# Layer 1's output projection: half of its inputs by seven products of block pairs for eight

## The chip, the cores and the metric

One core of one Trainium2 chip runs the whole kernel. The metric is the device time of one execution in microseconds. The engines are PE (TensorE, matmuls), PEld (its weight loads), DVE (VectorE), ACT (ScalarE), POOL (GpSimd) and SP (SyncE, which here only issues DMAs).

## What is computed

Two layers on x (1024 positions by 1024 channels), then a final RMSNorm. The change lies in layer 1, the pooling mixer, and there in its last product:

```python
def odd_mixer(h, w_in, w_grp, b_grp, scale, w_out):
    proj = h @ w_in                      # 1024 -> 2 * 2048
    v, g = jnp.split(proj, 2, axis=-1)
...
    mixed = jnp.einsum('bsgc,gcd->bsgd', pooled - vg, w_grp).reshape(bsz, s, POOL_WIDTH) + b_grp
    y = mixed * scale * jax.nn.silu(g)
    return y @ w_out                     # (1024 x 2048) @ (2048 x 1024)
...
        x = x + gate[:, None, :] * y
    return rmsnorm(x, final_g)
```

y has four groups of four blocks of 128 channels. Below, block k of y is y[:, 128 k : 128 (k + 1)], held with its channels on the 128 partitions.

## The kernel before, in words

**Precision.** Every large product of float32 operands is made of three matmuls in float32r: each operand is split into an upper part (ACT, a copy that rounds, `..._hi`) and a lower part (DVE, operand less upper part, `..._lo`), and hi·hi, hi·lo and lo·hi are summed in PSUM (`products`, L2190 to L2195). "A matmul" below is one of the three, 128x128 by 128x512.

**Seven products.** Most of the input projections are already made by pairs of column blocks with a scheme of seven products for eight (`pair`, `product`): the 1024 inputs are halved into even and odd 128-blocks (4 of each, KP = 4), the 1024 positions into two halves. The moving side X, in SBUF for the whole layer, holds four blocks of h and three sums T1, T2, T3 (T4 takes B12's place later), each hi and lo. The stationary side of a pair comes from two loaded blocks of weights (`R1`, `R2`): POOL makes four sums (`sums_of_weights`), ACT and DVE split them (`prep(q, idx)`, in slots of a ring w_hi/w_lo of six 512-wide places). A product is 4 x 3 = 12 matmuls. Product 4 of a pair runs after product 1 of the next (`last_of`). ACT and DVE add up the products from PSUM (`take_1`, `add_11` and so on).

**Layer 1's output projection.** The 16 blocks of y are written to DRAM (`spill_y`) as the four groups are finished, in the order 0, 3, 2, 1. Then come two passes, A over the row blocks b = 0 to 3 and B over b = 4 to 7. A pass has 16 steps, one for each block k of y: SP loads 128 rows of w_out into the ring `raw` (`ring_load`, four places) and half of block k of y (`y_load`), ACT and DVE split both (`step_splits`), and PE runs 4 row blocks x 2 halves of the columns x 3 matmuls = 24 matmuls, y stationary, the weights moving. All eight PSUM banks gather a pass. The last two steps of pass A (three of pass B) are run row block by row block, so that the banks fill one after the other. `residual(1, b)` (DVE) multiplies a row block by the gate and adds it to x, four operations of 512 columns for a row block; `squares`, `inverse` and `row_out` make the final norm; `store` writes the rows.

**What sets the order.** All engines run instruction lists written out by hand, with semaphores. Every engine takes its list in order, so that what waits holds back all behind it. A split may be made when its ring place is free: the place of step n's weights is that of step n - 3 (`E_LAST`, `w_used`), and y's upper part has three places (YS). PE counts `o_step` at the last row block of a step. In pass A of before DVE's list at the turn to pass B reads:

```python
                        if layer == 1 and p == "B":
                            if at == 1:
                                residual(1, 0)
                                residual(1, 1)
                                residual(1, 2)
                            if at == 2:
                                residual(1, 3)
                        step_splits(y_step)
```

Of the kernel before, what the change touches and what calls it, by code (L numbers as in the profile page):

```python
# [10 lines left out]
P = 128  # L11
# [8 lines left out]
GB = 4  # L20
# [20 lines left out]
for _name, _n in ROWS_A + ROWS_B:  # L41
# [14 lines left out]
PAIRS += [(name, n) for n in range(GROUPS) for name in ("V01", "G01", "V23", "G23") if n or name[1] == "2"]  # L56
Q = {pair: q for q, pair in enumerate(PAIRS)}

# [6 lines left out]
        if PAIRS[q] != ("C", HEADS - 1) and not (PAIRS[q][0] == "V01")}  # L65
TIME_ORDER = [k + half * KB for k in range(KB) for half in range(2)]
GROUP_ORDER = [GB * g + m for g in GORDER for m in range(GB)]
# [3 lines left out]
           1: {b: (2 * (b % 4), 2 * (b % 4) + 1) for b in range(SB)}}  # L71
# [39 lines left out]
def build(nc, x, c, norm_g, mod_w, mod_b, hy_w_in, hy_conv_w, hy_conv_b, lru_w_a, lru_b_a, lru_w_x, lru_b_x,  # L111
# [41 lines left out]
    def last_steps(layer, p):  # L153


        blocks, steps = BLOCKS[layer, p], list(range(2 * KB - LAST[layer, p], 2 * KB))
# [30 lines left out]
    for q in range(3 * (HEADS - 1)):  # L187
        add_pair(q)
    STEPS = [(layer, p, k) for layer, p in BLOCKS
             for k in ((TIME_ORDER if layer == 0 else GROUP_ORDER) if p == "A" else range(2 * KB))]  # L190
    mods1 = [("m1", chunk, kk) for kk in range(KB) for chunk in range(2)]
    for layer in range(2):
        if layer == 1:
# [38 lines left out]
    with ExitStack() as ctx:  # L232
# [67 lines left out]

        def flat(ap):
# [55 lines left out]
        def piece(at, width, dt=F32):  # L357
            if dt is F32R:
# [124 lines left out]
        half_done = sem("half_done")  # L483

# [53 lines left out]
        def dst_free(q, which):  # L538
# [28 lines left out]
        def _(sp):  # L567
# [25 lines left out]
            def ring_load(unit):  # L593
# [9 lines left out]
                if kind in ("R1", "R2"):  # L603
                    name, n = PAIRS[unit[1]]
                    which = "R1 R2".split().index(kind)
                    if name in PAIR_L0:
# [44 lines left out]
            def y_load(step):  # L651
# [3 lines left out]
                if Y[step] >= YR:  # L655
                    sp.wait_ge(ylo_done, Y[step] - YR + 1)
                if p == "A":
# [1920 lines left out]
```

## Time and profile before

| | us |
|---|---|
| median of 3 runs | 1303.23 |
| lowest and highest run | 1301.58, 1304.64 |
| the profiled execution, its own time | 1303.3 |
| its span in the trace | 1301.5 |
| PE busy | 1278.2 (98%) |
| DVE, ACT, POOL busy | 938.1, 629.3, 273.0 |

The span begins with the first instruction and ends with the last store; the execution's own time is 1.8 us more. In the page PE's busy time counts a matmul of 512 columns as 0.39 us, though the next one starts 0.227 us after it: they overlap, so the pace is read from starts and not from durations. A row of a timeline gives the start, the duration, the engine, the line, and in brackets how long the engine was idle before it and what ended that.

### The profile page before, as it was taken

How to read it: one execution, taken by the hardware profiler on the slowest of the kernel's cores; microseconds unless marked ns; L12 is line 12 of the kernel's file. 1: busy time of each engine (PE TensorE's matmuls, PEld its weight loads, DVE VectorE, ACT ScalarE, POOL GpSimd, SP SyncE). 2: the span in 40 equal slices, each digit the busy share in tenths (PEclk: the TensorE clock that was granted, in tenths of full speed). 3: DMA queues.
4: the chain of work that ended last, by engine and by line, in shares of the span. 5: the costliest groups of instructions: out<-in, count | busy, mean ns of one | idle time of the engine just before them, and what ended most of it. 6: DMA issues, size and time to landing. Idle time of an engine off the chain costs nothing.

```text
span 1301.5 us, 15429 instructions
## 1 busy us (share of the span) xinstructions
PE 1278.2 (98%) x5687; PEld 1055.3 (81%) x5687; DVE 938.1 (72%) x1119; ACT 629.3 (48%) x888; POOL 273.0 (21%) x158
## 2 busy tenths in 40 slices
PE   6999999999999999999999999999999999999997
PEld 5877888888888888888888888888888888888886
DVE  6889987878878887778477698758758656434636
ACT  7466656464646464545567574144144143222522
POOL 0033443443524332000000023133133131000000
PEclk8999999999999999999999999999999999999999
DMA  9712233323232341698748202321321321874441
GB/s 290 218 49 69 89 110 97 104 67 113 69 114 73 110 134 45 223 380 269 268 165 267 81 18 79 101 79 34 112 82 34 112 81 39 309 243 145 177 155 65
DMA packets 145618, 171.51 MB, mean 132 GB/s; under 512 B 6598, under 2 KB 117382, under 8 KB 145544
## 3 DMA queue, kind: packets, MB, share of 16 engines
q1 hardware_dynamic: 145544, 170.53, 40.6%
q8 instruction: 46, 0.75, 0.2%
q14 instruction: 28, 0.23, 0.1%
HBM read 145.33 MB, written 25.17 MB: 131 GB/s over the span
## 4 chain that ended last, share of the span: by engine, by line
PE 88%; DVE 7%; SPq 2%; issue 1%; ACT 1%; DMA 0%; DVEq 0%; ACTq 0%
PE psum L2193 29%; PE psum L2195 29%; PE psum L2194 29%; SPq L587 1%; DVE whole_x L1863 1%; DVE w_lo L1410 1%; DVE X L1500 1%; PE psum L2328 1%; DMA late<-in_mod_w 0%; SPq L576 0%; ACT w_hi L879 0%; DVE bufs L1645 0%; DVE w_lo L1432 0%; DVE late L1493 0%; PE psum L2334 0%
## 5 line engine op out<-in xcount | busy, mean ns | idle before, releaser
L2193 PE MATMUL psum<-X,w_hi 128*128 128x512 f32 x1140 | 446.3, 391 | 2.6 <-DVE X L1544 2.2
L2194 PE MATMUL psum<-X,w_hi 128*128 128x512 f32 x1140 | 444.4, 390 | 0.0
L2195 PE MATMUL psum<-X,w_lo 128*128 128x512 f32 x1140 | 444.3, 390 | 0.0
L2193 PEld LDWEIGHTS psum<-X,w_hi 128*128 128x128 f32 x1140 | 214.5, 188 | 49.4 <-DVE X L1544 2.8
L2195 PEld LDWEIGHTS psum<-X,w_lo 128*128 128x128 f32 x1140 | 214.4, 188 | 44.9
L2194 PEld LDWEIGHTS psum<-X,w_hi 128*128 128x128 f32 x1140 | 214.5, 188 | 44.3 <-issue 0.2
L1410 DVE TENSOR_TENSOR w_lo<-raw,w_hi 128x1024 fp32r<-128x1024 f32 x98 | 120.5, 1231 | 156.4 <-ACT w_hi L879 156.0
L879 ACT ACTIVATE w_hi<-raw 128x1024 fp32r<-128x1024 f32 x98 | 103.6, 1057 | 201.6 <-PE psum L2195 159.9
L901 ACT ACTIVATE w_hi<-ssum 128x512 fp32r<-128x512 f32 x140 | 87.1, 626 | 120.3 <-PE psum L2195 91.1
L1432 DVE TENSOR_TENSOR w_lo<-ssum,w_hi 128x512 fp32r<-128x512 f32 x140 | 119.9, 863 | 22.1 <-ACT w_hi L901 21.4
L840 POOL TENSOR_TENSOR ssum<-raw 128x512 f32<-128x512 f32 x35 | 62.6, 1790 | 287.5 <-DMA raw<-in_pool_w_in 253.7
L848 POOL TENSOR_TENSOR ssum<-ssum,raw 128x512 f32<-128x512 f32 x35 | 55.8, 1595 | 309.4 <-DVE w_lo L1432 309.4
L2193 PE MATMUL psum<-w_hi,X 128*128 128x512 f32 x256 | 99.7, 389 | 0.3 <-DVE whole_x L1867 0.3
L2195 PE MATMUL psum<-w_hi,X 128*128 128x512 f32 x256 | 99.6, 389 | 0.0
L2194 PE MATMUL psum<-w_lo,X 128*128 128x512 f32 x256 | 99.6, 389 | 0.0
L851 POOL TENSOR_TENSOR ssum<-raw 128x512 f32<-128x512 f32 x35 | 78.5, 2244 | 78.7 <-DVE w_lo L1432 78.7
L845 POOL TENSOR_TENSOR ssum<-ssum,raw 128x512 f32<-128x512 f32 x35 | 62.1, 1774 | 47.1 <-DVE w_lo L1432 45.1
L1424 DVE TENSOR_TENSOR w_lo<-raw,w_hi 128x1024 fp32r<-128x1024 f32 x35 | 42.7, 1220 | 24.7 <-ACT w_hi L890 24.5
L2193 PEld LDWEIGHTS psum<-w_hi,X 128*128 128x128 f32 x256 | 48.0, 188 | 10.7 <-DVE whole_x L1867 0.7
L2195 PEld LDWEIGHTS psum<-w_hi,X 128*128 128x128 f32 x256 | 48.0, 188 | 10.0
L2194 PEld LDWEIGHTS psum<-w_lo,X 128*128 128x128 f32 x256 | 48.0, 188 | 9.9
L2193 PE MATMUL psum<-d_hi,w_hi 128*128 128x512 f32 x128 | 49.9, 390 | 0.3 <-DVE w_lo L1410 0.3
(244 smaller groups left out, 1955.0 us busy)
## 6 DMA issues: line engine op xcount, KB each, us to landing
raw<-in_hy_w_in SPq DMA_DIRECT2D x48, 512.0 KB, 5.2
raw<-in_hy_w_out SPq DMA_DIRECT2D x48, 512.0 KB, 4.9
raw<-in_pool_w_in SPq DMA_DIRECT2D x32, 512.0 KB, 5.1
raw<-in_pool_w_out SPq DMA_DIRECT2D x32, 512.0 KB, 4.1
aux<-in_mod_w SPq DMA_DIRECT2D x16, 512.0 KB, 4.0
y_dram<-bufs SPq DMA_DIRECT2D x16, 512.0 KB, 2.6
raw<-in_mod_w SPq DMA_DIRECT2D x16, 512.0 KB, 5.9
y_dram<-gb_ SPq DMA_DIRECT2D x16, 512.0 KB, 3.3
```

The lines of the kernel that those rows point to most:

```text
L840: nc.gpsimd.tensor_tensor(even, a21, a22, ALU.add).then_inc(s_ready, 1)
L845: nc.gpsimd.tensor_tensor(odd, even, a11, ALU.add).then_inc(s_ready, 1)
L848: nc.gpsimd.tensor_tensor(even, odd, a12, ALU.add).then_inc(s_ready, 1)
L851: nc.gpsimd.tensor_tensor(odd, a21, a11, ALU.add).then_inc(s_ready, 1)
L879: nc.scalar.activation(flat(w_hi[:, es:es + 2, :]), raw[:, at, :], ACT.Copy).then_inc(hi_done, 1)
L901: nc.scalar.activation(w_hi[:, es, :], ssum[:, op % 2, :], ACT.Copy).then_inc(hi_done, 1)
L1410: nc.vector.tensor_tensor(flat(w_lo[:, es:es + 2, :]), raw[:, at, :], flat(w_hi[:, es:es + 2, :]).bitcast(F32), ALU.subtract).then_inc(lo_ ...
L1424: ins = nc.vector.tensor_tensor(w_lo[:, es:es + 2, :].rearrange("p two (k n) -> p two k n", k=KP), raw_blocks(q, 0), w_hi[:, es:es + 2, :] ...
L1432: ins = nc.vector.tensor_tensor(w_lo[:, es, :], ssum[:, op % 2, :], w_hi[:, es, :].bitcast(F32), ALU.subtract)
L2193: nc.tensor.matmul(out_, whi, xhi, start=first, stop=False, skip_group_check=check)
L2194: nc.tensor.matmul(out_, whi, xlo, start=False, stop=False, skip_group_check=check)
L2195: return nc.tensor.matmul(out_, wlo, xhi, start=False, stop=last, skip_group_check=check)
```

## The change

Layer 1's output projection is split by inputs. Blocks k = 0 to 3 and 12 to 15 of y (the two groups that are finished first) go on as steps, so that each pass has 8 steps. Blocks 4 to 11 go by four pairs of row blocks (`("O", j)`, j = 0 to 3, rows 256 j to 256 j + 255) with the scheme of seven products. The stationary side is now y (R1 and R2 are two row blocks of the eight y blocks, read back from DRAM), and the moving side are 1024 rows of w_out, loaded into X's place when h is no longer needed, with the same seven blocks. The pairs run between pass A and pass B. Pair j yields rows 2j and 2j + 1 complete over these inputs; `add_rows` multiplies them by the gate and adds them to x's rows. What the two passes yield is added by `residual` as before.

With it goes: POOL makes T1 and T3 of the resident weights and DVE T2 and T4 (8 operations each, 512 wide); ACT and DVE split them in eight operations each, 2048 and 1536 wide (`upper_out`, `low_out`), put between the splits of pass A's steps; y's halves get places of their own (`y_raw1`, `y_hi1`, and `y_lo1` in y_raw1's place), so `y_load` waits for PE to have used a place (`o_step`) and no longer for DVE; SP loads the eight blocks of w_out (512 KB each) after the weights of the steps 1 and 2; the spills of the last group, the gate's row and x's rows move.

```diff
-GROUP_ORDER = [GB * g + m for g in GORDER for m in range(GB)]
+GROUP_ORDER = [GB * g + m for g in GORDER[:2] for m in range(GB)]
+PAIRED = range(GB, GB + KB)
+N_STEPS = (2 * KB, KB)
...
@@ SP
+            def out_weights(kp):
+                sp.wait_ge(full_of["4"], OUT)
+                for n in range(2):
+                    k = PAIRED[2 * kp + n]
+                    sp.dma_start(whole_x[kp][:, 2 * n:2 * n + 2, 1, :],
+                                 w_out[1][k * P:(k + 1) * P, :].rearrange("p (two n) -> p two n", two=2))\
+                      .then_inc(out_in[kp], 16)
+            for n, step in enumerate(s for s in STEPS if s[0] == 1 and s[1] == "A"):
                 ring_load(("W",) + step)
                 y_load(step)
+                if n in (1, 2):
+                    for kp in (2 * n - 2, 2 * n - 1):
+                        out_weights(kp)
...
@@ ACT
+            for n, step in enumerate(s for s in STEPS if s[0] == 1 and s[1] == "A"):
+                if n < 2:
+                    continue
+                step_splits(step)
+                if n in (2, 3, 4, 5):
+                    upper_out(n - 2)
+            load_root()
+            first_operands(OUT)
...
@@ DVE
+            for n, step in enumerate(s for s in STEPS if s[0] == 1 and s[1] == "A"):
+                if n < 2:
+                    continue
+                step_splits(step)
+                if n in (2, 3, 4, 5):
+                    t2_and_t4_out(n - 2)
+                    if n > 2:
+                        low_out(n - 3)
+            low_out(KP - 1)
+            first_operands(OUT)
+            residual(1, 0)
+            residual(1, 1)
+            prep(OUT, 0)
+            residual(1, 2)
...
@@ PE
                 if q >= 2:
                     pe.wait_ge(neg21, q - 1)
+                if q == OUT:
+                    pe.wait_ge(out_lo, 2 * KP)
+                    pe.wait_ge(o_evac, o_count(1, 1, 1))
                 product(q, "1")
...
+                if q == OUT:
+                    pe.wait_ge(o_evac, o_count(1, 2, 1))
...
+                if (layer, p) == (1, "B"):
+                    for q in range(OUT, len(PAIRS)):
+                        pair(q, after_1=(lambda: last_of(q - 1)) if q > OUT else None)
```

ACT's list in pass A, before. L879 is the upper split of a step's weights, L946 that of y; o_step is PE's count of finished steps.

```order
L879 ACTIVATE w_hi<-raw 128x1024 [waits psum_full,raw_in2]
L946 ACTIVATE X<-whole_x 128x512 [waits o_step,y_in2]
L879 ACTIVATE w_hi<-raw 128x1024 [waits o_step,raw_in3]
L946 ACTIVATE X<-whole_x 128x512 [waits o_step,y_in3]
L879 ACTIVATE w_hi<-raw 128x1024 [waits o_step,raw_in0]
```

The same place now. L961 and L1030 are the same two splits, L1469 the splits of the resident weights (`upper_out`), which wait for the sums of POOL (t13_added) and DVE (t24_added).

```order
L961 ACTIVATE w_hi<-raw 128x1024 [waits psum_full,raw_in2]
L1030 ACTIVATE y_hi<-y_raw 128x512 [waits gate_done,o_step,y_in2]
L1469 ACTIVATE X<-whole_x 128x4x512 [waits t13_added,t24_added]
L1469 ACTIVATE X<-whole_x 128x3x512
L961 ACTIVATE w_hi<-raw 128x1024 [waits o_step,raw_in3]
L1030 ACTIVATE y_hi<-y_raw 128x512 [waits o_step,y_in3]
L1469 ACTIVATE X<-whole_x 128x4x512 [waits t13_added,t24_added]
```

Two wide operations that wait for DVE now stand between the splits of two steps. On DVE each step's splits are followed by T2 and T4 (L2296, L2300), for which ACT's next wide operations wait, and then by the two wide lower splits of the group before (L2308).

DVE's list at the end of pass A, before (L1863 and L1867 are `residual`, L1410 and L1477 the splits of pass B's steps 0 and 1):

```order
L1410 TENSOR_TENSOR w_lo<-raw,w_hi 128x1024 [waits hi_done]
L1477 TENSOR_TENSOR X<-whole_x,X 128x512 [waits yhi_done]
L1863 TENSOR_TENSOR whole_x<-psum,whole_x 128x512 [waits psum_full,gate_in]
L1867 TENSOR_TENSOR whole_x<-whole_x 128x512 [waits xr_in0,part_made]
L1863 TENSOR_TENSOR whole_x<-psum,whole_x 128x512 [waits psum_full]
L1867 TENSOR_TENSOR whole_x<-whole_x 128x512 [waits xr_in0,part_made]
```

And now (L1546 and L1554 are the lower splits of operands 0 and 2 of the first pair, L1985 and L1989 `residual`):

```order
L1546 TENSOR_TENSOR w_lo<-raw,w_hi 128x1024 [waits hi_done]
L1554 TENSOR_TENSOR w_lo<-ssum,w_hi 128x512 [waits hi_done]
L1985 TENSOR_TENSOR d_sums<-psum,d_sums 128x512 [waits psum_full,gate_in]
L1989 TENSOR_TENSOR gb_<-gb_,d_sums 128x512 [waits xr_in0,part_made]
L1985 TENSOR_TENSOR d_sums<-psum,d_sums 128x512 [waits psum_full]
L1989 TENSOR_TENSOR gb_<-gb_,d_sums 128x512 [waits xr_in0,part_made]
```

The split of operand 2 now stands ahead of the first `residual`. By the ring (`E_LAST`) operand 2 takes the place of the weights of step 6, the last but one of pass A, so that its upper part waits for PE's count of that step.

## Rows read from the trace of the kernel before

**Rows 1.** The page, parts 1 and 4: busy time, and the chain by engine
```profile
PE 1278.2 (98%) x5687; PEld 1055.3 (81%) x5687; DVE 938.1 (72%) x1119; ACT 629.3 (48%) x888; POOL 273.0 (21%) x158
...
PE 88%; DVE 7%; SPq 2%; issue 1%; ACT 1%; DMA 0%; DVEq 0%; ACTq 0%
```

**Rows 2.** Windows: us of each engine (instructions), clock, DMA share, GB/s
```profile
1110.00:1197.00 87.00, 87.00 (x385) 72.07 (x384) 32.69 (x36) 26.49 (x34) 0.00 (x0) 1.00 0.68 242
1295.00:1302.00 7.00, 0.00 (x0) 0.00 (x0) 3.53 (x6) 1.44 (x6) 0.00 (x0) 0.63 0.41 160
```

**Rows 3.** PE timeline, last group's mix and product 4: start us, us, what
```profile
1099.80 0.39 PE L2193 MATMUL psum<-X,w_hi 128*128 128x512 f32 x1
...
1102.52 0.39 PE L2193 MATMUL psum<-d_hi,w_hi 128*128 128x512 f32 x1
```

**Rows 4.** ACT timeline, pass A, with idle before and its releaser
```profile
1119.10 1.06 ACT L879 ACTIVATE w_hi<-raw 128x1024 fp32r<-128x1024 f32 x1 [7.81 <-PE psum L2195]
1120.06 0.61 ACT L946 ACTIVATE X<-whole_x 128x512 fp32r<-128x512 f32 x1
1124.54 1.06 ACT L879 ACTIVATE w_hi<-raw 128x1024 fp32r<-128x1024 f32 x1 [3.86 <-PE psum L2195]
```

**Rows 5.** DVE timeline, start of pass A
```profile
1119.04 1.28 DVE L2045 SCALAR_TENSOR_TENSOR gb_<-psum,vec,gb_ 128x1024 f32<-128x1024 f32 x1 [3.76 <-PE psum L2195]
1120.24 1.22 DVE L1410 TENSOR_TENSOR w_lo<-raw,w_hi 128x1024 fp32r<-128x1024 f32 x1
1121.37 0.68 DVE L1477 TENSOR_TENSOR X<-whole_x,X 128x512 fp32r<-128x512 f32 x1
```

**Rows 6.** Line 1493, T2 sums of layer 1: ns min/median/max, first and last start
```profile
L1493 DVE SCALAR_TENSOR_TENSOR d_sums<-d_sums,whole_x x4: 691/691/693, 743.4 to 756.5; 128x512 f32<-128x512 f32 x4
```

**Rows 7.** ACT, DVE and PE timelines, end of pass A and start of pass B
```profile
1205.46 1.06 ACT L879 ACTIVATE w_hi<-raw 128x1024 fp32r<-128x1024 f32 x1 [8.62 <-PE psum L2195]
...
1198.09 0.68 DVE L1863 TENSOR_TENSOR whole_x<-psum,whole_x 128x512 f32<-128x512 f32 x1
...
1203.40 0.68 DVE L1863 TENSOR_TENSOR whole_x<-psum,whole_x 128x512 f32<-128x512 f32 x1
...
1210.42 0.40 PE L2195 MATMUL psum<-w_hi,X 128*128 128x512 f32 x1
1211.08 0.50 PE L2193 MATMUL psum<-w_hi,X 128*128 128x512 f32 x1 [0.27 <-DVE whole_x L1867]
```

**Rows 8.** POOL and DVE timelines, one stretch in which both are busy
```profile
1013.05 1.29 POOL L840 TENSOR_TENSOR ssum<-raw 128x512 f32<-128x512 f32 x1 [10.49 <-DMA raw<-in_pool_w_in]
...
1013.50 1.92 DVE L1410 TENSOR_TENSOR w_lo<-raw,w_hi 128x1024 fp32r<-128x1024 f32 x1 [0.49 <-ACT w_hi L879]
1015.35 0.67 DVE L1461 TENSOR_TENSOR vp<-vp,psum 128x512 f32<-128x512 f32 x1
```

**Rows 9.** Windows (columns as in rows 2) and PE timeline: the clock falls and rises
```profile
22.00:24.00 2.00, 0.72 (x5) 0.72 (x6) 1.41 (x4) 0.00 (x0) 0.00 (x0) 0.92 1.10 312
32.00:34.00 2.00, 2.00 (x6) 1.52 (x6) 1.23 (x6) 1.53 (x2) 0.00 (x0) 0.52 1.18 292
1296.00:1297.00 1.00, 0.00 (x0) 0.00 (x0) 1.00 (x1) 0.81 (x3) 0.00 (x0) 0.92 0.00 0
...
23.28 0.69 PE L2390 MATMUL psum<-ones,macc 128*128 128x1 f32 x4 [2.52 <-DVE macc L1525]
...
29.92 0.79 PE L2193 MATMUL psum<-X,w_hi 128*128 128x512 f32 x1 [0.83 <-DVE X L1544]
...
33.92 0.39 PE L2193 MATMUL psum<-X,w_hi 128*128 128x512 f32 x1
```

**Rows 10.** DMA issues of the page and SP timeline: loads for layer 1's projection
```profile
raw<-in_pool_w_out SPq DMA_DIRECT2D x32, 512.0 KB, 4.1
...
1102.77 0.34 SPq L664 DMA_DIRECT2D whole_x<-y_dram  x1
```

More of the change, by code:

```diff
@@ L153, in last_steps @@
     def last_steps(layer, p):
-        blocks, steps = BLOCKS[layer, p], list(range(2 * KB - LAST[layer, p], 2 * KB))
+        blocks, steps = BLOCKS[layer, p], list(range(N_STEPS[layer] - LAST[layer, p], N_STEPS[layer]))
         order = [(n, b, half) for b in blocks for half in range(2) for n in steps]
@@ L483, in build @@
         half_done = sem("half_done")
+        out_in = [sem(f"out_in{kp}") for kp in range(KP)]
+        out_hi = sem("out_hi")
+        out_lo = sem("out_lo")
+        pair_part = sem("pair_part")
+        pair_added = sem("pair_added")
         def v(name, n=0, count=1):
@@ L654, in y_load @@
                 at = Y[step] % YR
[L655 removed]
+                if Y[step] >= YR and layer == 0:
                     sp.wait_ge(ylo_done, Y[step] - YR + 1)
+                elif layer and Y[step] - YR >= Y[1, "A", GROUP_ORDER[0]]:
+                    sp.wait_ge(o_step, Y[step] - YR + 1)
                 if p == "A":
@@ L945, in split_y @@
                 width = slice(0, cols.stop - cols.start)
-                nc.scalar.activation(Y_HI[layer][n % YS][:, width], Y_RAW[layer][n % YR][:, width], ACT.Copy)\
-                  .then_inc(yhi_done, 1)
+                if (n - Y[1, "A", GROUP_ORDER[0]]) in range(YS):
+                    act.wait_ge(gate_done, GB * GROUPS)
+                nc.scalar.activation(y_hi(step)[:, width], y_raw(step)[:, width], ACT.Copy).then_inc(yhi_done, 1)
             def step_splits(step):
@@ new lines, in low_out, with add_rows @@
+            def low_out(kp):
+                for n, blocks in enumerate((slice(0, 4), slice(4, 7))):
+                    dve.wait_ge(out_hi, 2 * kp + n + 1)
+                    nc.vector.tensor_tensor(X[:, kp, blocks, 1, :], whole_x[kp][:, blocks, 1, :],
+                                            X[:, kp, blocks, 0, :].bitcast(F32), ALU.subtract).then_inc(out_lo, 1)
+            def add_rows(q, which):
+                b = 2 * (q - OUT) + which
+                part = dst(q)[which]
+                if which:
+                    second_complete(q)
+                else:
+                    first_complete(q)
+                nc.vector.tensor_tensor(part, part, gate1, ALU.mult).then_inc(pair_part, 1)
+                dve.wait_ge(pair_part, b + 1)
+                dve.wait_ge(xr_in[b % 4], 16 * (2 + b // 4 + 1))
+                nc.vector.tensor_tensor(XR[1][b], XR[1][b], part, ALU.add).then_inc(pair_added, 1)
@@ new lines, in _ @@
+            last = [s for s in STEPS if s[0] == 1 and s[1] == "B"]
+            for q in range(OUT, len(PAIRS)):
+                if q > OUT:
+                    take_22(q - 1)
+                    prep(q, 0)
+                prep(q, 1)
+                if q == OUT:
+                    residual(1, 3)
+                else:
+                    add_rows(q - 1, 0)
+                prep(q, 2)
+                prep(q, 3)
+                add_11(q)
+                if q > OUT:
+                    add_rows(q - 1, 1)
+                prep(q, 4)
+                prep(q, 5)
+                if q == len(PAIRS) - 1:
+                    step_splits(last[0])
+                add_12(q)
+                prep(q, 6)
@@ L2180, in _ @@
+            take_22(len(PAIRS) - 1)
+            step_splits(last[1])
+            for n, step in enumerate(last):
+                if n < 2:
+                    add_rows(len(PAIRS) - 1, n)
+                else:
+                    step_splits(step)
+                if n in (3, 4, 5, 6):
+                    row_out(n - 3)
             residual(1, 4)
@@ L2551, in _ @@
                     part_of(y_steps[n], b, half)
-                for n in range(ends, 2 * KB):
+                for n in range(ends, N_STEPS[layer]):
                     behind(layer, p, n)
```

198 lines of the change are left out of this document (142 added, 56 removed).

## The prediction

> **What bounds the kernel now.** I read the busy times and the chain first: PE is busy for 98% of the span and makes 88% of the chain that ends last [rows 1]. So a matmul taken away is worth its pace, and anything that makes PE wait costs its full length. The pace comes from the starts: product 4, 12 matmuls, begins at 1099.80 and the next mix at 1102.52 [rows 3], which is 2.72 us, or 0.227 us for a matmul. A step of a pass (24 matmuls) is then 5.44 us, and ACT's first split of a step comes exactly so often, at 1119.10 and 1124.54 [rows 4]. The windows show that in pass A PE runs without a gap (87.00 of 87 us) at full granted clock, with DVE busy for 32.7 us, ACT for 26.5 us and POOL for nothing [rows 2]: there is room beside PE. The one gap near the change is at the first step of pass B: PE starts at 1211.08 where it would have started at 1210.42 + 0.23 [rows 7], so 0.43 us are lost to `residual(1, 3)`.
>
> **What goes.** Half the inputs cost 2 passes x 8 steps x 24 = 384 matmuls; four pairs of 84 make 336. The 48 fewer are worth 48 x 0.227 = 10.9 us. The gap of 0.43 us goes too, since row block 3 is then evacuated long before pass B. Gain: 11.3 us. The tail after the last matmul, in which PE has no work [rows 2], keeps its instructions.
>
> **What comes, first place: pass A.** It starts at 1102.52 + 72 x 0.227 = 1118.84 (three mixes after rows 3) and has 8 steps. Between the splits of two steps ACT now has two wide copies that wait for DVE's T4, DVE's T2 and T4 come behind the step's lower splits, and these wait for ACT. That is a ring of waits, and I add it up:
> - ACT's copies take 0.61 us for 512 and 1.06 us for 1024 columns [rows 4], so 0.45 us for 512 more: 1.96 us for 2048 and 1.51 for 1536. Consecutive ones overlap by 0.1 us (1119.10 + 1.06 against 1120.06). The two wide ones hold ACT for 3.27 us, then the step's weights take 1.06.
> - DVE's splits take 1.73 us from start to the next start (1.13 between rows 5's last two starts, then some 0.6), and T2 and T4, each waiting for the one before, 2 x 0.69 [rows 6] and 0.06 for the hand-overs. With 0.03 us between the engines a round is 3.27 + 1.06 + 1.73 + 1.44 + 0.04 = 7.5 us, while PE needs only 5.44.
> - The first T4 ends at 1120.24 + 1.73 + 1.42 = 1123.4 [rows 5]. Three rounds later, at 1146.0, the last does. Then the wide copies, the weights of step 6 (ACT) and both lower splits (DVE): ready at 1146.0 + 3.27 + 1.06 + 0.03 + 1.13 + 0.68 = 1152.2. PE wants step 6 at 1118.84 + 6 x 5.44 = 1151.5 and waits 0.7. It wants step 7 three matmuls (0.68 us) later, for the last two steps are interleaved, but DVE ends step 7's splits 1.73 us after those of step 6: another 1.05. Sum 1.8 us. Steps 2 to 5 are in time by 1.5 us or more.
> - A lower end is 0, if wide copies cost less per column than narrow ones. At the upper end POOL's sums are still running at 1120 and hold up DVE's first splits: up to 4 us in all.
>
> **Second place: the first pair.** DVE's list has the lower split of operand 2 ahead of `residual(1, 0)`, and the upper part waits for PE to count step 6, the last but one matmul triple of the pass. In before the same release is seen: ACT's split starts at 1205.46, 0.42 us before pass A's end at 1118.84 + 16 x 5.44 = 1205.88 [rows 7]. From the end of pass A, then: ACT -0.42 to +0.19, DVE's split from +0.22, the first `residual` from +0.82, eight operations with the pace of rows 7 (1198.09 to 1203.40, 5.31 us), the last of them complete at +6.2. PE's product 1 of the first pair waits for the second of these row blocks (its bank), so PE stands still for 6.3 us. In before this work lay beside pass B's first step; here nothing covers it. POOL adds to it: as soon as operand 2's split is done it starts the next sum, and where POOL and DVE run together a DVE operation with two inputs from SBUF took 1.92 us [rows 8] instead of 1.22 [rows 5], while one that reads PSUM was not slowed (0.67). I take one such clash, 0.65 us. Sum: 6.9 us, bounds 6.3 (no clash) and 7.6 (two). The Trainium skill (SBUF — State Buffer, on the shared port pair) says that the pair is an exclusive lock for the whole instruction; the 0.7 us in the row agree with it, as POOL's operation ends at 1014.34 and DVE's 1.1 us later. By that rule a clash can cost up to POOL's whole 1.29 us, and the place would cost 7.6.
>
> **Third place: the clock.** After 2.5 us without work, PE's granted clock fell in the window 22 to 24 (mean 0.92, and then 0.5, which is 1.2 GHz), and at the end it fell in 1296 to 1297 (0.92), some 3 us after the last matmuls [rows 9]. A stall of nearly 7 us will do the same. When dense matmuls came back at 29.92 the level of 2.4 GHz returned at 33.92 [rows 9]: 4.0 us, half of which is lost, 2.0 us. The lower end is 1.1: if the clock stays up, product 1 lasts 2.7 us and product 2 waits for the third `residual` and its two hand-overs, which at the lower level are hidden. The upper end is half of the time that the clock was low at the start, 23.7 to 33.9, so 5.1.
>
> **What is hidden.** The eight loads of the resident weights are issued from 1102.8 on, when SP is released [rows 10], 4 MB. At the 290 GB/s and more that windows of this trace show [rows 9] they need some 14 us; the first T1 and T3 have until 1122, the others until 1129, 1137 and 1144. DVE's wide lower splits (3.9 us a round) lie beside ACT's 4.3. The pairs need for DVE some 8 us of lower splits and sums plus 4.6 us for `add_rows` in 19 us, for ACT 7, for POOL 6 to 8. The read-back of y by 512 B pieces has 15 us and more. Pass B's first y waits for the third pair's `add_rows` and is ready 3 us before PE wants it; its spacing after that is that of before. If any of these covers fails, it shows as a PE gap at that place.
>
> **Sum.** 11.3 - (1.8 + 6.9 + 2.0) = 0.6 us of gain. From the profiled execution, 1303.3 us (0.07 us above the median of the three runs), this gives 1302.7 us. A measurement of this kernel can tell about 0.2%, 2.6 us, from no change: I forecast no difference.
>
> **Rivals.**
> 1. *The small prices are smaller.* Wide copies are cheap, no clash, the clock stays up: 6.3 + 1.1 + 0 = 7.4 lost, 1303.3 - 3.9 = 1299.4. For it: room on both engines. Against it: both falls of the clock in rows 9. Chance 0.13.
> 2. *The wait for the first pair does not exist*, because the split of operand 2 is released earlier than I read from the ring. Then only pass A's 1.8 remain: 1303.3 - 11.3 + 1.8 = 1293.8. Against it: the same release is in rows 7. Chance 0.05.
> 3. *Slower: the ring of waits in pass A is longer.* It goes through ACT and DVE four times, so each microsecond more in a round costs up to four. If the wide operations, of which no row exists, cost half as much again as I worked out (1.6 us a round), PE loses 1.8 + 6.4: 1309.1. It decides from 0.8 us a round on, which takes the time past 1305.9. For it: no operation of that width in the trace. Against it: 512 to 1024 columns is linear. Chance 0.11.
> 4. *The clock stays low longer*, as at the start, 10 us: 3.1 us more than I take, 1305.8. Chance 0.12.
>
> That the matmuls are not saved can be set aside: the lists have 48 fewer. My own case has 0.59.
>
> **Numbers.** The own case spans 1300.6 to 1305.3. Faster by over 0.2% (below 1300.6): rival 2 and most of rival 1, 0.17. Slower by over 0.2% (above 1305.8): rival 3, half of rival 4, a tail of my case, 0.19. Within: 0.64. The range 1299.8 to 1306.3 leaves out rival 2, most of rival 3 and the end of rival 1.
>
> **What would show it.** In the profile after: 5639 PE instructions; a PE gap of 6 to 8 us at about 1164, ended by DVE's `residual` (L1989); ahead of it the row of operand 2's split (L1554) and not a PSUM wait; two small gaps at 1151 to 1154 ended by a DVE split; a window behind 1170 with the clock under 1. I am wrong if the big gap is missing, if PE waits in steps 2 to 5 of pass A, or if gaps stand between the pairs or at the start of pass B.

## The result, and the profile after

The changed kernel takes 1309.85 us (median of 7 runs, 1307.57 to 1312.33) against 1304.00 (7 runs beside it, 1301.58 to 1305.25): ratio 1.0041, interval 1.0032 to 1.0050. It is slower by 0.4%, 7.2 us above the 1302.7 that I predicted and above the range's upper end of 1306.3.

The profiled execution is the median run, 1309.85 us, with a span of 1308.1. The page after, parts 1 and 4, to hold against [rows 1]:

```profile
PE 1274.1 (97%) x5639; PEld 1049.6 (80%) x5639; DVE 987.6 (75%) x1155; ACT 641.8 (49%) x904; POOL 312.1 (24%) x182
...
PE 85%; DVE 8%; issue 2%; ACT 2%; SPq 1%; DMA 1%; DVEq 0%; ACTq 0%
```

48 matmuls fewer (5639 for 5687), and PE's share of the chain fell from 88% to 85%. So the matmuls went, and more than their time came as waiting. Where it lies is seen in the starts of PE's matmuls. First the kernel before: the first matmul of the last group's mix (four times 24 matmuls, with product 4 behind the first 24), and the last matmul of all:

```profile
1094.22 0.50 PE L2193 MATMUL psum<-d_hi,w_hi 128*128 128x512 f32 x1 [0.33 <-DVE w_lo L1410]
...
1293.28 0.39 PE L2195 MATMUL psum<-w_hi,X 128*128 128x512 f32 x1
```

The same two places after, and between them the starts behind the gaps:

```profile
1095.21 0.50 PE L2381 MATMUL psum<-d_hi,w_hi 128*128 128x512 f32 x1 [0.33 <-DVE w_lo L1532]
...
1147.81 0.47 PE L2381 MATMUL psum<-w_hi,y_hi 128*128 128x512 f32 x1 [0.28 <-DVE y_lo L1599]
...
1156.90 0.76 PE L2381 MATMUL psum<-w_hi,y_hi 128*128 128x512 f32 x1 [3.37 <-DVE y_lo L1599]
...
1158.64 0.77 PE L2381 MATMUL psum<-w_hi,y_hi 128*128 128x512 f32 x1
...
1177.80 0.77 PE L2381 MATMUL psum<-X,w_hi 128*128 128x512 f32 x1 [6.85 <-DVE gb_ L1989]
...
1299.81 0.39 PE L2383 MATMUL psum<-w_hi,y_lo 128*128 128x512 f32 x1
```

From mix to last matmul it is 199.06 us before and 204.60 after: 5.5 us more. Up to the start of the mix the ten kernels below have the changed kernel's own instructions, and yet it lies anywhere from 1093.99 (e1) to 1096.67 (e3) in their profiles, so that the 1.0 us of this pair says nothing. With the 11.3 us of gain, 16.8 us were lost, where I had 10.7. By starts (distance to the matmul before, less 0.23) it is 0.44 us at 1147.81, 3.53 at 1156.90, 0.52 at 1158.64, 7.01 at 1177.80 and 0.25 at 1114.63, 11.75 in all. The other 5.05 us are pace. Windows after (columns as in [rows 2]), from the gap before step 6 on, and from the one before the first pair:

```profile
1153.00:1157.00 4.00, 0.63 (x4) 0.24 (x2) 3.70 (x3) 3.97 (x7) 3.04 (x2) 0.84 0.71 262
1157.00:1159.00 2.00, 1.88 (x4) 1.09 (x5) 2.00 (x3) 0.71 (x1) 0.00 (x0) 0.50 0.64 189
1159.00:1162.00 3.00, 3.00 (x8) 2.32 (x8) 3.00 (x2) 0.00 (x0) 0.00 (x0) 0.50 0.58 174
1162.00:1164.00 2.00, 2.00 (x9) 1.57 (x9) 1.50 (x2) 0.00 (x0) 0.00 (x0) 0.87 0.00 0
1176.00:1178.00 2.00, 0.20 (x1) 0.23 (x2) 1.97 (x4) 0.00 (x0) 0.00 (x0) 0.55 0.00 0
1178.00:1182.00 4.00, 4.00 (x10) 3.13 (x11) 3.93 (x7) 0.00 (x0) 1.28 (x1) 0.50 0.01 2
1182.00:1184.00 2.00, 2.00 (x8) 1.55 (x8) 1.97 (x2) 0.76 (x2) 1.28 (x1) 0.75 0.02 4
```

The clock fell twice to 0.50 (1.2 GHz) and not once. In the first stretch 11 matmuls start late after the one before (mostly 0.43 us, the first ones behind a gap 0.56), in the second 12, for 0.227 at the other level: 23 x 0.2 = 4.6 us, and the longer first intervals bring the rest.

What makes step 6 late? POOL, ACT and DVE after, at the start of pass A:

```profile
1121.19 1.30 POOL L946 TENSOR_TENSOR whole_x<-whole_x 128x512 f32<-128x512 f32 x1 [1.22 <-DMA whole_x<-in_pool_w_out]
1122.45 2.28 POOL L948 TENSOR_TENSOR whole_x<-whole_x 128x512 f32<-128x512 f32 x1
```

```profile
1121.57 2.01 DVE L1532 TENSOR_TENSOR w_lo<-raw,w_hi 128x1024 fp32r<-128x1024 f32 x1
1123.50 1.77 DVE L1599 TENSOR_TENSOR y_lo<-y_raw,y_hi 128x512 fp32r<-128x512 f32 x1
...
1125.91 0.69 DVE L2300 SCALAR_TENSOR_TENSOR whole_x<-whole_x 128x512 f32<-128x512 f32 x1
```

```profile
1126.64 3.29 ACT L1469 ACTIVATE X<-whole_x 128x2048 fp32r<-128x2048 f32 x2 [4.63 <-DVE whole_x L2300]
...
1134.09 3.30 ACT L1469 ACTIVATE X<-whole_x 128x2048 fp32r<-128x2048 f32 x2 [2.70 <-DVE whole_x L2300]
...
1149.02 3.29 ACT L1469 ACTIVATE X<-whole_x 128x2048 fp32r<-128x2048 f32 x2 [2.70 <-DVE whole_x L2300]
```

The same two DVE splits took 1.22 and 0.68 us before [rows 5] and take 2.01 and 1.77 with POOL's T1 and T3 beside them. The first T4 (L2300) therefore ends 1.9 us late, and ACT's first wide copy waits for it. From there on the ring turns in 7.46 us (1126.64 to 1134.09, and from there to 1149.02 twice), which is the 7.5 that I had worked out; the two wide copies take 3.29 for 3.27. At step 6 POOL is there again, with the sums of the first pair:

```profile
1151.45 2.55 POOL L912 TENSOR_TENSOR ssum<-raw 128x512 f32<-128x512 f32 x1 [26.73 <-DMA raw<-y_dram]
1154.17 2.03 POOL L917 TENSOR_TENSOR ssum<-ssum,raw 128x512 f32<-128x512 f32 x1 [0.17 <-POOL ssum L912]
```

```profile
1153.30 1.79 DVE L1532 TENSOR_TENSOR w_lo<-raw,w_hi 128x1024 fp32r<-128x1024 f32 x1 [0.43 <-ACT w_hi L961]
1155.01 1.75 DVE L1599 TENSOR_TENSOR y_lo<-y_raw,y_hi 128x512 fp32r<-128x512 f32 x1
```

1.79 and 1.75 us for 1.22 and 0.68 make another 1.6 us. The gap before the first pair is the one that I described, with operand 2's split (L1554) ahead of the first `residual` and one clash (1.26 us for 0.69):

```profile
1170.97 0.69 DVE L1554 TENSOR_TENSOR w_lo<-ssum,w_hi 128x512 fp32r<-128x512 f32 x1 [7.48 <-ACT w_hi L983]
1171.58 0.68 DVE L1985 TENSOR_TENSOR d_sums<-psum,d_sums 128x512 f32<-128x512 f32 x1
1172.30 1.26 DVE L1989 TENSOR_TENSOR gb_<-gb_,d_sums 128x512 f32<-128x512 f32 x1
```

### The profile page after: what moved, and what is told of

It reads as the page before. It is cut to its first block, busy times and chain, and to the rows that moved or that the text cites. A ratio compares the mean times of both kernels' runs of the same rounds, so it can differ in the third digit from the quotient of the medians.

```text
span 1308.1 us, 15455 instructions
## 1 busy us (share of the span) xinstructions
PE 1274.1 (97%) x5639; PEld 1049.6 (80%) x5639; DVE 987.6 (75%) x1155; ACT 641.8 (49%) x904; POOL 312.1 (24%) x182
## 4 chain that ended last, share of the span: by engine, by line
PE 85%; DVE 8%; issue 2%; ACT 2%; SPq 1%; DMA 1%; DVEq 0%; ACTq 0%
PE psum L2381 28%; PE psum L2382 28%; PE psum L2383 28%; DVE w_lo L1532 1%; DVE whole_x L1985 1%; ACT w_hi L961 1%; DVE X L1622 1%; SPq L626 1%; DMA raw<-in_hy_w_out 1%; PE psum L2528 1%; DMA raw<-in_hy_w_in 0%; ACT X L1469 0%; SPq L615 0%; DVE y_lo L1599 0%; DVE w_lo L1554 0%
## 5 line engine op out<-in xcount | busy, mean ns | idle before, releaser
L2381 PE MATMUL psum<-X,w_hi 128*128 128x512 f32 x1252 | 491.4, 392 | 8.9 <-DVE gb_ L1989 6.8
L2382 PE MATMUL psum<-X,w_hi 128*128 128x512 f32 x1252 | 489.3, 391 | 0.0
L2383 PE MATMUL psum<-X,w_lo 128*128 128x512 f32 x1252 | 489.1, 391 | 0.0
L2381 PEld LDWEIGHTS psum<-X,w_hi 128*128 128x128 f32 x1252 | 236.4, 189 | 60.8 <-issue 9.0
L2383 PEld LDWEIGHTS psum<-X,w_lo 128*128 128x128 f32 x1252 | 236.3, 189 | 49.5
L2382 PEld LDWEIGHTS psum<-X,w_hi 128*128 128x128 f32 x1252 | 236.4, 189 | 48.8 <-issue 0.2
L1554 DVE TENSOR_TENSOR w_lo<-ssum,w_hi 128x512 fp32r<-128x512 f32 x156 | 130.8, 846 | 31.1 <-ACT w_hi L983 30.5
L961 ACT ACTIVATE w_hi<-raw 128x1024 fp32r<-128x1024 f32 x82 | 86.5, 1056 | 109.8 <-PE psum L2383 67.8
L1546 DVE TENSOR_TENSOR w_lo<-raw,w_hi 128x1024 fp32r<-128x1024 f32 x39 | 47.6, 1221 | 25.5 <-ACT w_hi L972 25.2
L2381 PE MATMUL psum<-w_hi,y_hi 128*128 128x512 f32 x128 | 51.1, 399 | 3.8 <-DVE y_lo L1599 3.6
L2382 PE MATMUL psum<-w_lo,y_hi 128*128 128x512 f32 x128 | 50.8, 397 | 0.0
L2383 PE MATMUL psum<-w_hi,y_lo 128*128 128x512 f32 x128 | 50.7, 396 | 0.0
L2150 DVE SCALAR_TENSOR_TENSOR gb_<-gb_,vec,win 128x1024 f32<-128x1024 f32 x16 | 20.5, 1284 | 39.0 <-ACT win L1361 39.0
L2382 PE MATMUL psum<-d_lo,w_hi 128*128 128x512 f32 x128 | 49.8, 389 | 0.0
L2383 PE MATMUL psum<-d_hi,w_lo 128*128 128x512 f32 x128 | 49.8, 389 | 0.0
```

The source lines that it names most:

```text
L961: nc.scalar.activation(flat(w_hi[:, es:es + 2, :]), raw[:, at, :], ACT.Copy).then_inc(hi_done, 1)
L1546: ins = nc.vector.tensor_tensor(w_lo[:, es:es + 2, :].rearrange("p two (k n) -> p two k n", k=KP), raw_blocks(q, 0), w_hi[:, es:es + 2, :] ...
L1554: ins = nc.vector.tensor_tensor(w_lo[:, es, :], ssum[:, op % 2, :], w_hi[:, es, :].bitcast(F32), ALU.subtract)
L2381: nc.tensor.matmul(out_, whi, xhi, start=first, stop=False, skip_group_check=check)
L2382: nc.tensor.matmul(out_, whi, xlo, start=False, stop=False, skip_group_check=check)
L2383: return nc.tensor.matmul(out_, wlo, xhi, start=False, stop=last, skip_group_check=check)
```

## The experiments

Each kernel was run 5 times, e2, e3, e5 and e6 11 times. Below, "mix to end" is the distance from the first matmul of the last group's mix to the last matmul in its profile, free of what lies ahead (before: 199.06, after: 204.60), and "slow" counts matmuls that start 0.38 to 0.57 us after the one before, most of them 0.43. The columns of the profile tell of one execution, which is not always the median one: it took 1306.70 us for e2, 1305.82 for e5, 1305.34 for e6 and 1295.70 for e9.

| kernel | median us | ratio to before (interval) | mix to end | gaps at steps 5, 6, 7 | slow | gap at first pair | slow |
|---|---|---|---|---|---|---|---|
| the change | 1309.85 | 1.0041 (1.0032-1.0050) | 204.60 | 0.44, 3.53, 0.52 | 11 | 7.01 | 12 |
| e1 | 1298.95 | 0.9959 (0.9946-0.9971) | 194.92 | 0.27, 3.57, 0.81 | 5 | none | 0 |
| e2 | 1305.12 | 1.0007 (0.9996-1.0019) | 201.81 | 0, 2.54, 0 | 7 | 7.00 | 11 |
| e3 | 1304.97 | 1.0007 (0.9998-1.0016) | 198.68 | 0, 0.58, 0.96 | 0 | 7.00 | 9 |
| e4 | 1295.42 | 0.9928 (0.9916-0.9941) | 189.49 | 0, 0.36, 0 | 0 | 0.85 | 0 |
| e5 | 1306.64 | 1.0022 (1.0012-1.0031) | 201.49 | 0, 2.22, 0.97 | 0 | 7.00 | 10 |
| e6 | 1306.82 | 1.0016 (1.0007-1.0025) | 201.08 | 0.31, 1.93, 0.97 | 0 | 7.03 | 12 |
| e7 | 1294.46 | 0.9923 (0.9910-0.9937) | 190.05 | 0, 0.37, 0 | 0 | 0.87 | 0 |
| e8 | 1298.01 | 0.9951 (0.9939-0.9964) | 193.72 | 0, 0.59, 0.97 | 0 | 2.33 | 8 |
| e9 | 1293.73 | 0.9923 (0.9909-0.9937) | 189.19 | 0, 0.50, 0 | 0 | 0.85 | 0 |
| e10 | 1309.16 | 1.0037 (1.0025-1.0050) | 204.39 | 0, 2.99, 0.97 | 13 | 7.00 | 14 |

### e1: residuals ahead of operand 2's lower split

```diff
-            first_operands(OUT)
-            residual(1, 0)
-            residual(1, 1)
+            lo(OUT, 0)
+            for b in range(3):
+                residual(1, b)
+            lo(OUT, 2)
             prep(OUT, 0)
-            residual(1, 2)
```

> DVE takes the first three residuals of row block 0's evacuation ahead of operand 2's lower split; they wait for pass A's banks, which close long before its end. Theory A (the stall of 6.85 us at the junction is the list order of DVE, and the low clock behind it, 12 matmuls at the lower level, is the stall's doing): the gap at 1177 falls below 1 us and the clock stays at 1 there; -7.0 for the wait and -2.5 for the clock: 9.5 us less than the changed kernel's 1309.85, so 1300.3. Theory B (the wait is real, but the clock would fall anyway, or another wait, of product 1 for its bank, takes the place of this one): at most -3 to -7, so 1303 to 1307, with a new gap between 1170 and 1178. The two gaps of the ring (0.3 and 3.4 us at 1148 and 1153) stay in either.

Measured 1298.95 us; the ratio is 0.8% below the changed kernel's. The 7.01 us of waiting and the 2.5 us of pace at the first pair are gone, which is theory A's 9.5. That mix to end fell by as much (9.7) is in part luck: 1.2 us less of low clock behind step 6 and 0.9 us more of waiting at 1114 nearly cancel. DVE's timeline of e1:

```profile
1162.98 0.68 DVE L1985 TENSOR_TENSOR d_sums<-psum,d_sums 128x512 f32<-128x512 f32 x1
...
1170.93 1.29 DVE L1554 TENSOR_TENSOR w_lo<-ssum,w_hi 128x512 fp32r<-128x512 f32 x2
```

The first `residual` starts 8.6 us earlier than in the changed kernel (1162.98 for 1171.58), 7.4 us when both are counted from the mix, beside pass A's last matmuls, and operand 2's split is still in time. No gap and no slow matmul is left at the first pair. The order of one operation in DVE's list cost 7.0 us of waiting, and the wait brought 2.5 us of low clock.

### e2: the ring of waits opened

```diff
-                if n in (2, 3, 4, 5):
-                    upper_out(n - 2)
+                if n in (3, 4, 5, 6):
+                    upper_out(n - 3)
...
                     t2_and_t4_out(n - 2)
-                    if n > 2:
-                        low_out(n - 3)
-            low_out(KP - 1)
+                if n > 3:
+                    low_out(n - 4)
```

> The last wide copies of each group of w_out move one step later on ACT, and the wide lower splits another step on DVE, so no round of ACT and DVE waits for itself. Theory A (the ring of waits sets pass A's steps 5 to 7): the gaps at 1147.8 and 1153.5 go, -4.3 us, and the clock does not fall at 1157, -2.65: 1302.9. Theory B (POOL's sums beside DVE's splits are what is late, the ring only passes it on): the splits of the weights still take 1.7 to 2.0 us, a gap of 1 to 2 us stays in steps 5 to 7: 1304 to 1307. The stall of 7 us at the junction stays in either.

Theory B: 1305.12 us, and a gap stays before step 6, of 2.54 us and not 1 to 2. ACT's wide copies come 5.44 us apart, so the ring is open. POOL and DVE of e2 show what is late now:

```profile
1149.76 1.58 POOL L912 TENSOR_TENSOR ssum<-raw 128x512 f32<-128x512 f32 x1 [25.23 <-DMA raw<-y_dram]
1151.51 2.58 POOL L917 TENSOR_TENSOR ssum<-ssum,raw 128x512 f32<-128x512 f32 x1 [0.17 <-POOL ssum L912]
```

```profile
1147.91 5.05 DVE L2308 TENSOR_TENSOR X<-whole_x,X 128x2048 fp32r<-128x2048 f32 x2
1152.88 2.30 DVE L1532 TENSOR_TENSOR w_lo<-raw,w_hi 128x1024 fp32r<-128x1024 f32 x1
```

The pair of wide splits takes 5.05 us where it takes 3.95 elsewhere in this profile, and the step's split 2.30 for 1.22: each lost 1.1 us to one POOL instruction.

### e3, e5 and e6: POOL's sums put where they meet nothing

e3 has both waits, e5 the first, e6 the second:

```diff
             for kp in range(KP):
                 pool.wait_ge(out_in[kp], 32)
+                if kp == KP - 1:
+                    pool.wait_ge(t24_added, 2 * 2 * KP + 2)
...
+            pool.wait_ge(ylo_done, Y[1, "A", GROUP_ORDER[-1]] + 1)
             for q in range(OUT, len(PAIRS)):
                 sums_of_weights(q)
```

> The work of DVE and ACT is as in the changed kernel; POOL alone waits: for T1 and T3 of the last group until DVE has added the first T2 and T4, and for the pairs' sums until pass A's last lower split. Theory A (of the 4.3 us lost in pass A 3.5 are the two clashes with POOL, the ring by itself the 0.7 to 1.8 of my forecast): DVE's splits at 1121 and 1153 fall from 2.01, 1.77, 1.79 us to 1.2 and 0.7, the gap at 1153 falls from 3.37 to below 1.2 us, and the clock stays up: -3.5 - 2.65 = 1303.7. Theory B (DVE's splits are slow there for another reason, such as the loads that land at the same time): durations and gap stay, and the time stays at 1309.8.

> Only the first of e3's two waits: POOL's T1 and T3 of the last group of w_out wait until DVE has added the first T2 and T4; the pairs' sums run as they come. Theory A (each clash has its own price, and a wait of more than some 2.5 us brings the clock down): DVE's splits at the start of pass A take 1.2 and 0.7 us, all rounds of the ring come 1.8 us earlier, the gap before step 6 is 3.4 - 1.8 = 1.6 us, and the clock stays up: 1309.85 - 1.8 - 0.4 - 2.65 = 1305.0. Theory B (the clock falls for 1.6 us too): 1307.6. Theory C (only the second clash counts): 1309.8.

> Only the second wait: the pairs' sums on POOL wait for pass A's last lower split. Theory A: DVE's split of step 6 takes 1.2 us for 1.8 to 2.3 and the wide split ahead of it 3.95 for 5.05, the gap before step 6 is 3.4 - 1.6 = 1.8 us, that of 0.3 us before step 5 stays, and the clock stays up: 1309.85 - 1.6 - 2.65 = 1305.6. Theory B (the clock falls for 1.8 us too): 1308.2. Theory C (only the first clash counts): 1309.8.

e3 took 1304.97 us, 1.3 above theory A's figure; mix to end fell by 5.92, where 6.15 was expected, although three slow matmuls fewer at the first pair helped. DVE's splits take what they take alone, and the clock stays up:

```profile
1122.99 1.22 DVE L1535 TENSOR_TENSOR w_lo<-raw,w_hi 128x1024 fp32r<-128x1024 f32 x1
1124.12 0.69 DVE L1602 TENSOR_TENSOR y_lo<-y_raw,y_hi 128x512 fp32r<-128x512 f32 x1
```

```profile
1154.81 0.47 PE L2384 MATMUL psum<-w_hi,y_hi 128*128 128x512 f32 x1 [0.42 <-DVE y_lo L1602]
...
1156.54 0.47 PE L2384 MATMUL psum<-w_hi,y_hi 128*128 128x512 f32 x1 [0.80 <-DVE y_lo L1602]
```

What is left before steps 6 and 7, 0.58 + 0.96 = 1.5 us, is the ring by itself; the forecast had 0.7 + 1.05. Nothing in ACT's or DVE's lists differs from the changed kernel, so the other 2.9 us of waiting were POOL's (some 3.4 at the steps 5 and 6; before step 7 the changed kernel waits 0.45 us less than e3, as its matmuls run at the low clock there).

e5 and e6 show the two prices apart. e6 takes 1.6 us off the gap before step 6 (3.53 to 1.93), exactly the second clash. In e5 the first wide copy starts 4.33 us after ACT's first split of pass A, in the changed kernel 6.21: the first clash is 1.9 us. Its gap came out at 2.22 and not at 1.6, because I had taken the clash from the gap before step 6 alone; the 0.44 of step 5 is the same lateness, so that 3.53 + 0.44 - 1.9 = 2.1 was to be expected. In the two profiles the clock stayed up behind gaps of 2.2 and 1.9 us, against theory B, and theory C fell in both.

Both medians, 1306.64 and 1306.82, lie 1.2 to 1.6 us above theory A. In the profiles I find this slip and a gap of 1.3 us ahead of pass A (e5), of which below, and the wait of 0.97 us before step 7, which the low clock had hidden in part (both). But e5's 11 runs reach from 1305.39 us at a mean granted clock of 0.990 to 1311.02 at 0.984, the profiled one has 0.990, and the kernel before stays within 0.991 to 0.994. So a further fall of the clock in other executions of e5 is likely, and theory B is refuted for the profiled execution only. e2's runs spread alike, from 1301.57 us at 0.991 to 1308.79 at 0.986. Where the clock fell in them no profile shows.

### e4: e1 and e2 together

> Both orders together: the first residuals ahead of operand 2's lower split, and the wide copies a step later. Theory A (the losses are 7.0 + 2.5 at the junction and 4.3 + 2.65 in pass A, and independent): 1309.85 - 16.5 = 1293.4, PE without a gap above 1 us from 1100 to 1299, faster than the kernel before by 0.8%. Theory B (the gain of the 48 matmuls is partly given back elsewhere, or each cure only moves the wait): 1297 to 1302, with new gaps in which DVE or ACT is late between 1150 and 1185.

1295.42 us, 0.7% below the kernel before. Mix to end fell by 15.1 of the 16.5 us. Left are 0.32 us at 1116, 0.36 at step 6 and, at the first pair, this:

```profile
1166.48 0.47 PE L2380 MATMUL psum<-X,w_hi 128*128 128x512 f32 x1 [0.69 <-DVE gb_ L1989]
```

DVE works without a pause from 1133.9 to 1170.1 here, and two of the four second operations (L1989) of the two row blocks that PE waits for take 1.07 us for 0.69, with POOL's second sum of the pair beside them: 0.75 of the 0.85 us. That sum is late because POOL's first one had to wait this time:

```profile
1152.02 9.30 POOL L912 TENSOR_TENSOR ssum<-raw 128x512 f32<-128x512 f32 x1 [25.91 <-DMA raw<-y_dram]
```

Alone such a sum takes 1.3 us. It came 2.5 us after the start of DVE's two wide splits (1149.48) and was done 9.3 us later. In e2, with the same lists up to there, it came 1.85 us after their start, got its turn behind the first of them, and DVE was held up instead: the 2.54 us of e2's gap are e4's 0.36 and two times 1.1. In e4 the sum's own 1.3 us begin at 1152.02 + 9.30 - 1.3 = 1160.0, when DVE takes its first operation with an input from PSUM (L1985, at 1160.09); five DVE instructions with two inputs from SBUF had started since POOL asked.

What decides between the two outcomes is open. The moment of asking alone does not: in e3, e6 and e8 POOL asked 0.15 to 0.17 us after the start of two such wide splits and had its turn behind the first, after 2 us, while in e7 and e9 it asked 0.16 us after their start and waited 4.8 us, again until the first operation that reads PSUM. DVE and POOL of e7:

```profile
1154.06 3.95 DVE L2311 TENSOR_TENSOR X<-whole_x,X 128x2048 fp32r<-128x2048 f32 x2
...
1159.06 0.68 DVE L1988 TENSOR_TENSOR d_sums<-psum,d_sums 128x512 f32<-128x512 f32 x1
```

```profile
1154.22 6.08 POOL L912 TENSOR_TENSOR ssum<-raw 128x512 f32<-128x512 f32 x1 [26.39 <-DVE y_lo L1602]
```

### e7 and e8: both orders with both waits, and the residuals first with both waits

> Both orders and both waits of POOL. Theory A (what e4 still loses to the changed kernel's own gain of 11.3 us, 0.4 us at the last steps of pass A and 0.85 at the junction, is POOL beside DVE): no gap above 0.3 us from 1100 to 1290, 1.0 us less than e4: 1294.4. Theory B (the second wait only shifts POOL's sums onto the residuals, which are on the path in this order): the gap at the junction grows to 1.5 to 2 us, 1296 to 1297.

> The residuals first and both waits of POOL, the ring left as it is. From the start of the last mix to the last matmul e3 took 198.7 us; its stall of 7.0 and the slow matmuls behind it, 1.8, go. Theory A (the ring alone costs the 1.5 us that e3 shows, and nothing more): 198.7 - 8.8 = 189.9 us from mix to end, 0.4 us more than e4: 1295.8. Theory B (with the junction's stall gone the ring's lateness comes back at the first pair, as the residuals now start behind late lower splits): 1297 to 1299, with a gap of 1 to 3 us at 1165 to 1170.

e7 took 1294.46 us (ratio 0.9923), which cannot be told from e4. That is theory A's figure, but by luck: the gap at the first pair stayed at 0.87, and 0.37 at step 6 and 0.89 at 1115 stayed too, so neither mechanism held, and mix to end is 0.6 us longer than e4's. POOL's second sum still costs two L1992 operations of the residuals 0.4 us each, as in e4.

In e8 theory B held in time and place, but its lateness is for the most part POOL's. The wait has moved POOL's sums behind step 7's splits, where they hold up DVE's pair of wide splits and operand 0's split, 1.1 us each (5.05 for 3.95, 2.31 for 1.22):

```profile
1153.93 5.05 DVE L2311 TENSOR_TENSOR X<-whole_x,X 128x2048 fp32r<-128x2048 f32 x2
1158.91 2.31 DVE L1549 TENSOR_TENSOR w_lo<-raw,w_hi 128x1024 fp32r<-128x1024 f32 x1
```

The residuals stand right behind them and come 2.33 us after PE wants them, 2.2 of which are this clash. PE and windows of e8:

```profile
1166.79 0.47 PE L2384 MATMUL psum<-X,w_hi 128*128 128x512 f32 x1 [2.18 <-DVE gb_ L1992]
```

```profile
1166.00:1168.00 2.00, 1.21 (x4) 1.06 (x5) 1.97 (x4) 0.00 (x0) 0.00 (x0) 0.85 0.00 0
1168.00:1170.00 2.00, 2.00 (x6) 1.54 (x6) 1.97 (x4) 0.00 (x0) 0.13 (x1) 0.50 0.01 4
```

Behind 2.33 us of waiting the clock fell; 8 slow matmuls followed. So the places are not independent: the same clash stands in e3 and e6 (5.05 and 2.31, 5.04 and 2.31), where it was hidden by the wait of 7 us.

### e9 and e10: POOL's sums of T1 and T3 in DVE's idle time

In all profiles up to here but that of the kernel before PE also waits at 1114 to 1116 (after 0.25, e1 1.15, e2 0.50, e3 0.20, e4 0.32, e5 1.29, e6 0.20, e7 0.89, e8 0.25 us), ahead of the last 24 matmuls of the last group's mix, for an evacuation by DVE (L2158). DVE after, at that place:

```profile
1110.32 1.27 DVE L1532 TENSOR_TENSOR w_lo<-raw,w_hi 128x1024 fp32r<-128x1024 f32 x1 [2.41 <-ACT w_hi L961]
1111.51 1.77 DVE L1599 TENSOR_TENSOR y_lo<-y_raw,y_hi 128x512 fp32r<-128x512 f32 x1
```

DVE's split of y takes 1.77 us there too, with POOL's T1 and T3 beside them. The edit of both kernels (e9 also has those of e7, with `kp == 2` for the first wait):

```diff
+            pool.wait_ge(ylo_done, Y[1, "A", GROUP_ORDER[1]] + 1)
             for kp in range(KP):
                 pool.wait_ge(out_in[kp], 32)
+                if kp == 2:
+                    pool.wait_ge(t24_added, 2 * 2 * KP + 2)
```

> Both orders as in e7; on POOL the first T1 and T3 now wait for DVE's lower split of pass A's second step (they run in DVE's idle time ahead of pass A), those of the third group for the first T2 and T4, the pairs' sums for pass A's last lower split. Theory A (the gap of 0.25 to 1.3 us at about 1114, before the last mix but one ends, which the kernel before does not have, is again POOL beside DVE's splits, which take 1.77 and up to 2.3 us there instead of 0.68 and 1.21): splits at 1110 to 1116 take 1.2 and 0.7 us, the gap of 0.9 us is gone, last mix to last matmul 190.05 - 0.9 = 189.2 us, about 1293.6. Theory B (the gap comes from elsewhere, such as the loads): it stays, 1294.5.

> The changed kernel's two lists of ACT and DVE; only POOL's T1 and T3 wait as in e9, the pairs' sums run as they come. Theory A (prices add up: first clash 1.9, ring and second clash stay): no gap at 1114, a gap of 2.1 us before step 6 and one of 1.0 before step 7, the clock stays up in pass A, junction 7.0 and its slow matmuls 2.2; last mix to last matmul 201.5 (e5) - 1.3 = 200.2 us, about 1305.3. Theory B (POOL's later sums delay ACT's wide copies): the gap before step 6 is above 3 us and the clock falls there: 1308 to 1310.

e9: 1293.73 us, mix to end 189.19 (189.2 expected), and the gap at 1114 is gone; DVE's split of y there takes 0.68 us:

```profile
1112.72 0.68 DVE L1603 TENSOR_TENSOR y_lo<-y_raw,y_hi 128x512 fp32r<-128x512 f32 x1
```

This is 0.77% below the kernel before (interval 0.6 to 0.9%) and the lowest median, but its ratio is that of e7, 0.9923: only the profiles tell the two apart. The sums of the last two groups now meet DVE at 1128 to 1132 (a split and a T2 of 0.69 us take 1.79 and 1.78), which PE does not see, as the ring is open.

e10: theory B, in time (1309.16) and mechanism. The gap at 1114 went, the one before step 6 grew to 2.99 us instead of 2.1, and the clock fell there. POOL's last sum now meets the split of the next round:

```profile
1128.48 1.32 POOL L951 TENSOR_TENSOR whole_x<-whole_x 128x512 f32<-128x512 f32 x1
```

```profile
1128.89 1.98 DVE L1535 TENSOR_TENSOR w_lo<-raw,w_hi 128x1024 fp32r<-128x1024 f32 x1 [4.31 <-ACT w_hi L964]
```

1.98 us for 1.22: 0.8 us, inside the ring, and so passed on to the end. Against e5 PE waited 0.8 us more at step 6 (and 1.3 less at 1114), yet mix to end is 2.9 us longer, because the clock fell at step 6 and stayed low for 14 matmuls instead of 10 at the first pair. Windows of e10 at step 6:

```profile
1157.00:1159.00 2.00, 1.60 (x4) 1.34 (x5) 2.00 (x2) 0.00 (x0) 0.00 (x0) 0.50 0.50 143
1159.00:1162.00 3.00, 3.00 (x9) 2.32 (x8) 3.00 (x3) 0.00 (x0) 0.00 (x0) 0.50 0.34 100
```

## Why the prediction was wrong

**What goes: right.** 48 matmuls and the gap of 0.43 us. In e9 the distance from mix to end is 9.9 us less than before; with its two gaps of 0.50 and 0.85 us, 11.2 us went, for the 11.3.

**Second place, the first pair: right.** 7.01 us for 6.9, at its place, by `residual`, behind operand 2's split, with one clash. All versions that keep the order show 7.0. Rival 2, that this wait does not exist, fell.

**First place, the ring in pass A: the term that failed.** The forecast took 1.8 us for it. The round (7.46 for 7.5) and the copies (3.29 for 3.27) were right, and e3 shows 1.5 us for the ring alone. But the changed kernel lost 4.5 us. The step reads "At the upper end POOL's sums are still running at 1120 and hold up DVE's first splits: up to 4 us in all", and I took 1.8, with nothing for POOL. The clash at 1120 happened (1.9 us), and a second one that I did not have at all, the pair's sums at 1151 to 1156 (1.6 us). All that was needed stood in [rows 8]: a DVE split with POOL beside it takes longer. I priced it at the first pair, where I knew that both ran, and not where the same two engines were given new work by the same change. The sign for being wrong that I had named, a wait of PE in steps 2 to 5, came at step 5 (0.44 us). Rival 3 comes near the measured time (1309.1 for 1309.85) by luck: its rounds would have lasted 1.6 us longer, and they lasted 7.46 us. The ring only passed on lateness from its first round, and more came at its end.

The Trainium skill (SBUF — State Buffer, SBUF: two separate sides) says that whichever of the two engines starts first has the pair for the whole instruction and the other fully blocks. The trace agrees with it in the prices, 1.1 us for a split that starts right behind a POOL sum of 1.3, and shows one thing beyond: in e4 POOL did not get its turn after one DVE instruction, but after several, 8 us later.

**Third place, the clock: half of it missing.** I had one fall, 2.0 us. The one at the first pair cost 12 x 0.2 = 2.4. The other, 11 slow matmuls or 2.2 us at step 6, followed from the wrong first term: behind e3's stalls of 0.58 and 0.96 us the clock stayed up, behind this one of 3.53 it fell. So the error of the first term was paid twice, 4.5 - 1.8 = 2.7 us in waiting and some 2.2 in clock. The whole of the pace was 5.05 us for 2.0. With 0.1 at the first pair and 0.25 before pass A the 6.1 us between 16.8 and 10.7 are complete: 2.7 + 3.05 + 0.1 + 0.25.

**Hidden work: right but for POOL.** No gap above 0.3 us stands between the pairs or in pass B, and the loads were in time. What was not hidden was POOL's work, which I had costed at nothing as "POOL 6 to 8" us: the time fits, but it does not lie beside DVE's.

## What to carry to other kernels

When a change gives POOL work of two SBUF inputs, look for every DVE operation of two SBUF inputs beside it, not only the one in mind: here each meeting cost DVE up to 1.1 us or POOL up to 8 us. A wait on POOL's side that moves its sums into DVE's idle time cost nothing (the first T1 and T3 in e9); one that moves them beside other DVE work moves the clash (e8, 2.2 us). Where an engine's list has an operation that waits for a late event ahead of one that is ready, the second pays (7 us here for one line). And price stalls of PE by what follows: in these profiles those up to 2.22 us cost their own length, and those of 2.33 to 7.03 us brought 5 to 14 matmuls at the lower clock with them, up to 2.9 us. That is one profile for each kernel, and e5's runs speak against a sharp edge.

## What was not expected of the hardware

- A POOL sum that takes 1.3 us alone took 9.3 us beside an unbroken run of DVE instructions (e4) and 6.08 us in e7 and e9, each time until DVE's first operation with an input from PSUM. In e2, where it came 0.7 us earlier in that run, DVE lost 1.1 us in each of two places instead.
- The clock fell after stalls of 2.33 us (e8) and 2.54 us (e2) and stayed up after 2.22 us (e5's profile). After nearly the same stall (3.53 and 3.57 us) 11 slow matmuls followed in one profile and 5 in another.
